# First norm of a two-block transformer step: its conditioning chunks in sixteen buffers, its tiles in PSUM, its time-step matmuls behind 24 units

## The reference

```python
c_act = jax.nn.silu(c)                       # c: (1, 1024)
mod = c_act @ ada_w + ada_b                  # ada_w: (1024, 6144)
sh1, sc1, gt1, sh2, sc2, gt2 = jnp.split(mod, 6, axis=-1)
h = rmsnorm(x, mix_pre_g) * (1.0 + sc1) + sh1
proj = h @ w_in                              # 1024 -> z, xbc, dt_raw, sc_b, sc_c, sc_h, gates
xbc = jax.nn.silu(causal_dwconv(xbc, conv_w, conv_b))
dt = jax.nn.softplus(dt_raw + dt_bias)       # 32 heads; the time step of the scan
```

## Time and profile before

| | us |
|---|---|
| median of 3 runs | 1198.6 (1196.49 to 1199.68) |
| profiled execution, its own time | 1196.25 |
| span of its profile | 1194.2 |
| TensorE matmuls busy | 1079.9 (90%) |
| TensorE weight loads busy | 999.0 (84%) |
| GpSimd busy | 722.9 (61%) |
| ScalarE busy | 637.1 (53%) |
| VectorE busy | 600.3 (50%) |
| mean granted TensorE clock | 0.95 of full speed |
| DMA, mean over the span | 189 GB/s |

### The profile page before, as it was taken

How to read it: one execution, slowest core, us unless ns; L and a number is a source line. 1 busy time by engine, 2 the same in 40 slices (tenths; PEclk the granted TensorE clock), 3 DMA queues, 4 the chain that set the end, 5 groups by cost and what they waited for, 6 DMA issues and landing times.

```text
span 1194.2 us, 22510 instructions
## 1 busy us (share of the span) xinstructions
PE 1079.9 (90%) x8161; PEld 999.0 (84%) x8161; DVE 600.3 (50%) x1193; ACT 637.1 (53%) x1106; POOL 722.9 (61%) x332
## 2 busy tenths in 40 slices
PE   3489999889899878999997899998979997999999
PEld 2389999878799867999996799995457586999998
DVE  5777524869964454555523441390137266444400
ACT  2445664255674356666545556736245545666642
POOL 0468888441248754888886387660860034888785
PEclk7699999999999988999998898999969998999999
DMA  8768877555546762777686287547320013555553
GB/s 309 283 214 280 275 278 255 186 201 195 153 148 230 264 212 73 238 225 236 218 263 228 66 272 256 179 129 301 140 72 1 1 58 109 188 181 188 177 184 115
DMA packets 63423, 226.26 MB, mean 189 GB/s; under 512 B 6880, under 2 KB 7936, under 8 KB 63104
## 3 DMA queue, kind: packets, MB, share of 16 engines
q1 hardware_dynamic: 62160, 221.20, 55.0%
q10 hardware_dynamic: 1200, 4.23, 1.1%
HBM read 224.32 MB, written 1.08 MB: 189 GB/s over the span
## 4 chain that ended last, share of the span: by engine, by line
PE 55%; issue 16%; POOL 15%; DVE 8%; ACT 4%; DMA 1%; POOLq 0%; ACTq 0%; DVEq 0%
PE psL L541 51%; POOL WL L468 14%; PE psO L541 3%; DVE CT L1752 1%; DVE CT L1764 1%; ACT R L1457 1%; DMA ring<-wts 1%; DVE adaring L1684 1%; DVE R L1671 1%; PE psS L541 1%; PE psS L872 1%; ACT L955 1%; DVE adaring L1685 0%; DVE X L1767 0%; DVE R L1670 0%
## 5 line engine op out<-in xcount | busy, mean ns | idle before, releaser
L468 POOL TENSOR_TENSOR WL<-ring,WH 128x1024 fp32r<-128x1024 f32 (+1 forms) x282 | 673.1, 2397 | 353.0 <-ACT WH L964 281.9
L541 PE MATMUL psL<-HR,WH 128*128 128x256 f32 x3056 | 557.4, 285 | 21.4 <-DVE HR L1537 8.0
L541 PEld LDWEIGHTS psL<-HR,WH 128*128 128x128 f32 x3056 | 475.4, 191 | 27.9 <-issue 15.9
L541 PE MATMUL psL<-HR,WL 128*128 128x256 f32 x1528 | 433.1, 283 | 0.0
L541 PEld LDWEIGHTS psL<-HR,WL 128*128 128x128 f32 x1528 | 292.1, 191 | 0.0
L964 ACT ACTIVATE WH<-ring 128x1024 fp32r<-128x1024 f32 (+1 forms) x210 | 216.1, 1040 | 142.1 <-PE psL L541 105.4
L541 PE MATMUL psL<-RR,WH 128*128 128x256 f32 x1344 | 241.9, 283 | 6.5 <-DVE RR L1730 3.6
L541 PEld LDWEIGHTS psL<-RR,WH 128*128 128x128 f32 x1344 | 207.6, 189 | 8.2 <-DVE RR L1730 4.0
L541 PE MATMUL psL<-RR,WL 128*128 128x256 f32 x672 | 189.3, 282 | 0.0
L1518 DVE SCALAR_TENSOR_TENSOR adaring<-adaring,psO 128x1024 f32<-128x1024 f32 x96 | 116.3, 1219 | 95.4 <-DMA adaring<-ada_w 86.6
L1793 DVE SCALAR_TENSOR_TENSOR CT<-psL,par,CT 128x254 f32<-128x254 f32 (+1 forms) x176 | 80.8, 480 | 121.7 <-ACT CT L1227 116.4
(11 more groups left out here) (244 smaller groups left out, 1125.6 us busy)
## 6 DMA issues: line engine op xcount, KB each, us to landing
ring<-wts SPq DMA_DIRECT2D x285, 512.0 KB, 4.1
adaring<-ada_w SPq DMA_DIRECT2D x96, 512.0 KB, 4.9
ring<-wts SPq DMA_DIRECT2D x16, 384.0 KB, 3.6
R<-cum_dram ACTq DMA_DIRECT2D x8, 512.0 KB, 4.9
WHF<-wts SPq DMA_DIRECT2D x2, 2048.0 KB, 8.4
ring<-wts SPq DMA_DIRECT2D x8, 288.0 KB, 2.7
WLF<-wts SPq DMA_DIRECT2D x1, 2048.0 KB, 13.7
ring<-wts SPq DMA_DIRECT2D x1, 2048.0 KB, 7.8
```

Source lines behind the costliest of these rows:

```text
L468: nc.gpsimd.tensor_tensor(WL[:, k, 0:n], ring[:, k, 0:n], WH[:, k, 0:n].bitcast(F32), SUB).then_inc(lo_done, 1)
L541: return nc.tensor.matmul(out, lhsT, rhs, start=start, stop=stop)
```

## The change

1. The first sixteen conditioning chunks go to sixteen places in R (`ADA0`), which is unused until the first unit's result, with a semaphore each; their loads wait for nothing. `adaring` serves chunks from 16 on, and 16 to 19 are loaded without a wait.
2. c is loaded broadcast to 128 partitions (`CROW`, 512 KB) and ScalarE writes silu of it to psO; the first diagonals and their matmuls are gone. Parameters are cut earlier: 192 columns (96 KB) first, the rest (1781.5 KB) later under a semaphore of its own.
3. SP's order at the start: CROW, first parameters, chunks 0 to 3, x, 4 to 9, weight 0, chunks 10 to 12, weight 1, chunks 13 to 15, weights 2 and 3, the other parameters, chunks 16 to 19, weights 4 to 7. Then conditioning chunk 20+k after weights 8+2k and 9+2k; the last rounds end with weights 60, 61, conditioning 46, weights 62, 63, conditioning 47.
4. `make_h` writes its scaled tile to one of three psL banks (1 to 3, `first_t`) and reads the root from psS. ScalarE makes two high halves before the tiles and two after.
5. The first units wait for the tiles k by k; the time-step matmuls stand behind unit 23, w_dt's halves behind the tiles, and VectorE's time-step chain behind the 24 convolutions, with conditioning steps 28 to 31 inside it.

```diff
+        ADA0 = [R[:, n * ADA_COLS + (0 if n < 14 else 4096):(n + 1) * ADA_COLS + (0 if n < 14 else 4096)] for n in range(ADA_FIRST)]
+        CROW = R[:, 20480:21504]
...
+        def first_t(j):
+            return psL[:, 1 + j % 3, 0:T]
...
-                if n >= ADA_SLOTS:
+                if n >= ADA_FIRST + ADA_SLOTS:
                     sp.wait_ge(ada_used, n - ADA_SLOTS + 1 + i * per)
...
+            sp.dma_start(CROW, c_row.rearrange("a b -> (a b)").partition_broadcast(P)).then_inc(c_in, 16)
             sp.dma_start(par[:, 0:PAR_FIRST], par_in[:, 0:PAR_FIRST]).then_inc(par_in_sem, 16)
             for n in range(4):
+                load_first(n)
+            sp.dma_start(X[:, :, :], x_t).then_inc(x_in, 16)
+            for n in range(4, 10):
+                load_first(n)
+            load(0)
+            for n in range(10, 13):
+                load_first(n)
+            load(1)
+            for n in range(13, 16):
+                load_first(n)
+            load(2)
+            load(3)
+            sp.dma_start(par[:, PAR_FIRST:NPAR], par_in[:, PAR_FIRST:NPAR]).then_inc(par2_in, 16)
+            for n in range(16, 20):
                 load_ada(n)
-            sp.dma_start(X[:, :, :], x_t).then_inc(x_in, 16)
-            for n in range(4, 16):
-                load_ada(n)
-            for c in range(SLOTS):
+            for c in range(4, 8):
                 load(c)
-            sp.dma_start(par[:, PAR_FIRST:NPAR], par_in[:, PAR_FIRST:NPAR]).then_inc(par_in_sem, 16)
-            load_ada(16)
-            load_ada(17)
             with sp.Fori(0, 7, 1) as i:
                 for k in range(4):
-                    load(4 + 2 * k, i, 8)
-                    load(5 + 2 * k, i, 8)
-                    load_ada(18 + k, i, 4)
-            for c in (60, 61):
-                load(c)
-            load_ada(46)
-            load_ada(47)
-            for c in (62, 63):
-                load(c)
+                    load(8 + 2 * k, i, 8)
+                    load(9 + 2 * k, i, 8)
+                    load_ada(20 + k, i, 4)
...
-            cond_rows(DIAG1, 1)
             pe.wait_ge(sq_ready, 1)
             stat("stat_mix", sq_at, 8)
+            linear8("in1", 0, 24, h_hi, h_lo, from_count(h_ready, 0))
             pe.wait_ge(wdt_ready, 1)
             out = scratch("dt")
             for k in range(KD):
-                pe.wait_ge(h_ready, k + 1)
                 wh, wl = (WDT[:, part, k * 32:(k + 1) * 32] for part in range(2))
                 last = triple(out[0:32, 0:T], wh, wl, HH[:, k, :], HL[:, k, :], k == 0, k == 7)
             last.then_inc(s_done, 1)
-            linear8("in1", 0, 64, h_hi, h_lo)
+            linear8("in1", 24, 40, h_hi, h_lo)
...
+            A(csil[:, :], pv("c_2"), ACT.Silu).then_inc(csil_ready, 1)
+            act.wait_ge(c_in, 16)
+            A(psO[:, :, :].rearrange("p a b -> p (a b)"), CROW, ACT.Silu).then_inc(cbc_ready, 1)
...
+            A(sbank("stat_mix")[:, 0:T], RS[:, 0, :], ACT.Exp, scale=-0.5).then_inc(rs_ready, 1)
+            for c in range(2):
+                high(c)
+            make_hh(mod[:, 0:8], 0, first_t)
+            for c in range(2, SLOTS):
+                high(c)
+            fed[0] = SLOTS
+            act.wait_ge(par2_in, 16)
+            A(WDT[:, 0, :], pv("w_dt"), ACT.Copy).then_inc(wdt_hi, 1)
...
+            units("in1", 24, 4, z_bank)
             act.wait_ge(dtw_ready, 1)
             A(dts[:, 4, :], dts[:, 2, :], ACT.Ln).then_inc(dtl_ready, 1)
+            units("in1", 28, 12, lambda k, u, i: z_bank(k, u, i, 4))
...
+            make_h(mod[:, 0:8], lead[:, 0:8], sbank("stat_mix")[:, 0:T], 0, first_t)
+            dve.wait_ge(t_ready, 8)
+            dve.sem_inc(s_free[SCRATCH["stat_mix"] % 2], 1)
+            dve.wait_ge(par2_in, 16)
             dve.wait_ge(wdt_hi, 1)
             V.tensor_tensor(WDT[:, 1, :], pv("w_dt"), WDT[:, 0, :].bitcast(F32), SUB).then_inc(wdt_ready, 1)
```

More of the change, by code:

```diff
@@ L39 @@
 ADA_COLS = 1024
-ADA_GROUPS = 6 * D // ADA_COLS
+ADA_FIRST = 16
 class Stream:
@@ L137 @@
 PAR_SPEC = [
-    ("c", 8), ("c_2", 8), ("ada_b", 48), ("mix_pre_g", 8), ("ones", P), ("ident", P), ("w_dt", KD * HEADS1),
-    ("mix_post_g", 8),
+    ("c_2", 8), ("ada_b", 48), ("mix_pre_g", 8), ("ones", P),
+    ("ident", P), ("w_dt", KD * HEADS1), ("mix_post_g", 8),
     ("xconv_w", 4 * NXBC), ("xconv_b", NXBC), ("dskip", 16), ("ssd_norm_g", 16), ("sconv_w", 24),
@@ L281, in build @@
         ada_arrived = [sem(f"ada_arrived{i}") for i in range(ADA_SLOTS)]
+        ada_first = [sem(f"ada_first{i}") for i in range(ADA_FIRST)]
         ada_used = sem("ada_used")
+        c_in, par2_in = sem("c_in"), sem("par2_in")
         diag_ready, cbc_ready, mod_ready = sem("diag_ready"), sem("cbc_ready"), sem("mod_ready")
@@ L1520, in _, with make_h @@
             dve.wait_ge(cbc_ready, 1)
-            for n, first in ((0, 8), (8, 0)):
-                with st.repeat(2, 0) as i:
-                    for kk in range(4):
-                        ada_step(n + kk, mod[:, bass.ds(i * 4 + (first + kk), 1)], i, 4)
-            def make_h(shift, gains, rs, base):
+            for n in range(ADA_FIRST):
+                first = n + 8 if n < 8 else n - 8
+                dve.wait_ge(ada_first[n], 16)
+                V.scalar_tensor_tensor(ADA0[n], ADA0[n], 1.0, cond, MUL, MUL, accum_out=mod[:, first:first + 1]
+                                       ).then_inc(ada_used, 1)
+            def make_h(shift, gains, rs, base, t_at=None):
+                slots = 3 if t_at else 4
                 for j in range(KD + 1):
                     if j < KD:
-                        if j >= 4:
-                            dve.wait_ge(h_ready, base + j - 3)
-                        V.scalar_tensor_tensor(CT[:, j % 4, :], X[:, j, :], gains[:, j:j + 1], rs, MUL, MUL
-                                               ).then_inc(t_ready, 1)
+                        if j >= slots:
+                            dve.wait_ge(h_ready, base + j - slots + 1)
+                        V.scalar_tensor_tensor(t_at(j) if t_at else CT[:, j % 4, :], X[:, j, :], gains[:, j:j + 1], rs, MUL,
+                                               MUL).then_inc(t_ready, 1)
                     if j >= 1:
@@ L1719, in _ @@
                 if m == 4:
-                    diagonals(DIAG2, 8)
+                    diagonals(DIAG2)
                 u = u0 + m
```

109 lines of the change are left out of this document (52 added, 57 removed).

## The result

| | before | after |
|---|---|---|
| median, measured together | 1199.14 us (1196.49 to 1202.33) | 1156.54 us (1153.14 to 1166.93) |
| profiled execution, its own time | 1196.25 us | 1153.14 us |
| span of its profile | 1194.2 us | 1151.2 us |

The ratio is 0.9662, with an interval of 0.9634 to 0.9689: 40.5 us gained by the ratio, 42.6 by the medians. The forecast was 1177.5 us, with a range of 1171 to 1188. The change has moved the code by some lines, so before's L541 is L554 in after, L468 is L481, L964 is L976, L1518 is L1542 for the first sixteen steps and L1536 for the rest, L1532 and L1537 are L1552 and L1557, and L1610 is L1632.

The account below looks back on a forecast made before the run. Matmuls into psL carry 51% of the span; gains were sought where TensorE is not streaming. Terms 13.1 + 5.9 - 2.8 + 3.7 = 19.9 us: 1176.4, or 1178.7 against the median; taken 1177.5, range 1171 to 1188.

Parts of the forecast that it names:

- 1, last early chunk: Start: conditioning chunk 15 usable at 31.0 instead of 32.94, with DMA at 405 GB/s; 1.9 us gained.
- 2, to the first tile: Between last early chunk and first tile: the time-step subtraction leaves the path; 0.3 us gained.
- 3, tiles: Normed tiles on VectorE: 7.1 us instead of 15.4, no low half beside them, one SBUF operand; 8.3 us gained.
- 3, last tile to unit 3: First unit follows the tiles k by k, 0.6 us behind the last instead of 2.84; 2.6 us gained.
- 4, units 3 to 23: in1 units until 24: TensorE's stall for VectorE's convolution and its slow clock go; 5.9 us gained.
- 5, units 23 to 60: 24 time-step matmuls now stand in a full stream behind unit 23; 2.8 us lost.
- 6, units 60 to 63: End of in1: weights 62 and 63 no longer queue behind conditioning load 47; 3.7 us gained, bounds 2.0 to 4.2.
- the late convolution: Rival: a third collision makes VectorE's first convolution late for unit 4; 3 us lost, 1181 us; chance 0.13.
- After in1 every stage should be the same and only shifted: Sign to look for: stages behind in1 keep their times, and the gain made before them stays.
- The slow feed: Rival: DMA at the start stays at the ring's 330 GB/s; gain 10 us, 1187 us; chance 0.20.
- The broadcast row: Rival, slower than before: the condition row's load, first in the queue, delays everything; 1217 us if it takes 40; chance 0.05.
- The gain is not kept: Rival: what comes early waits later for something that does not move; 1195 us; chance 0.04.

Follow-up runs that it names:

- f2: after with an unused tensor of 32 bytes per partition ahead of X, giving all but some small buffers before's addresses; 1179.19 us, ratio 0.9826.
- h3: f2 with before's load order at the end of in1: conditioning chunk 47 ahead of weight chunks 62 and 63; 1184.14 us, ratio 0.9899.
- D = 320 and 448: D: distance WH to HR modulo 512. 320: after with 128 bytes ahead of X, 1172.1 us; 448: before with 224 bytes, 1182.39 us, and i2.
- i1: after with 512 unused bytes per partition ahead of X; 1156.03 us, ratio 0.9638 to before.
- i2: after with 256 unused bytes per partition ahead of X; 1155.99 us in one run.

## Why the prediction was wrong, point by point

Of f2, which is the change at before's addresses, every term can be read from the last chunk's step, the first tile, the last low tile, the convolution starts of units 3 and 23 and the products of units 60 and 63:

| term | forecast | f2 | after |
|---|---|---|---|
| 1, last early chunk | 1.9 (at 31.0) | 2.1 (30.87) | 1.3 (31.64) |
| 2, to the first tile | 0.3 | 0.3 | 0.4 |
| 3, tiles | 8.3 | 8.5 | 8.5 |
| 3, last tile to unit 3 | 2.6 | 2.8 | 3.2 |
| 4, units 3 to 23 | 5.9 | 5.9 | 8.3 |
| 5, units 23 to 60 | -2.8 | -2.7 | 0.1 |
| 6, units 60 to 63 | 3.7 | 3.8 | 3.8 |
| sum, at the product of unit 63 | 19.9 | 20.7 | 25.5 |
| behind it | 0 | -2.3 | 17.6 |
| profiled execution | 1176.4 us | 1177.87 us | 1153.14 us |

- **Parts 1 to 4 held** in their sizes, each within 0.3 us in f2. Where I chose between bounds (405 GB/s between 330 and 413; no price for a PSUM operand; no price for weight 4 and the late convolution) the trace of after shows 404 to 429 from 9 us on, 0.47 to 0.48 us and no stall. The last early chunk starts between 30.29 and 31.82 in the fourteen kernels with this feed, and between 32.13 and 34.71 in five with before's: a spread that no part of the sum had, and which hides differences under 1.5 us. In part 3 the reason was only half the right one: the text names the low halves and the SBUF operands, and not the 4.13 us for which VectorE waited for ScalarE. The size came out because the 7.1 us of undisturbed tiles, read from the trace, left out both losses.
- **Part 5** is -2.7 as forecast. **Part 6** has the forecast size as a difference of two whole kernels, but only 2.3 of its 3.8 belong to the order of the last loads (h3); the rest came with something else in the change, which I did not follow. The forecast had put all of it down to the order, so its 3.7 is in part luck.
- **The step that failed** is one that was not a term of the sum: "After in1 every stage should be the same and only shifted", and with it the 2.84 us per unit that was carried over to every stage. I had read 460 matmuls in 54.2 us as what TensorE takes, a property of the instruction. It is one of several cadences: after has 2.72 us per unit. The diff had this in plain sight, as `("c", 8)` dropped from the parameter table, and I counted its bytes of DMA but not where the buffers behind it would go. The missing term is the 22.7 us between f2 and after; without it, 1179.19 stands against 1177.5, and in the range. (That f2 came so near is in part luck: of its 20.7 us at unit 63 the profiled execution loses 2.3 behind it, which the sum did not have either.)
- **The rivals.** The slow feed did not come (404 to 429 GB/s). The broadcast row was used at 5.95, near the 6 reckoned, but it was not free: from 3 to 9 us DMA moved 320 GB/s in after and 361 in f2, where before has 389. By an estimate, (389 - 320) x 6 us / 405, that is 1.0 us in after and 0.4 in f2. It is also most of the spread of the last early chunk: the six kernels that moved 319 to 338 GB/s in these 6 us have it at 31.45 to 31.82, and the eight with 351 to 368 at 30.29 to 30.98. The Trainium skill, "DMA: Bandwidth & Descriptors", section "Where 436 GB/s comes from", with its 358 GB/s for loads from HBM, is not what this trace of a single core shows; "Perfetto Trace Analysis", section "Roofline", which lets a single core draw up to about 435, agrees with 429. The late convolution is the rival that came nearest: two collisions, as reckoned (1.40 and 2.42 us), and unit 0's first tap at 45.74, where 45.9 was forecast. "The gain is not kept" did not come: 20.7 us at unit 63 are 18.4 at the end of f2, and 20.9 by its ratio.
- **Range and chances.** The range was built of feed, stalls and order, the resources that the diff names. No width of these holds a time that comes from the layout. The chance of 0.91 for faster came out, and the reason given for it covers half of the gain.

What stays open: what in the chip the distance of weights and tiles touches (TensorE's weight load against its own moving read, or reads of other engines beside them) was not separated; nor what picks the cadence at D = 320 and 448, where both are seen; nor whether 192 is fast with weights and tiles both elsewhere; nor whether RR, which moves along with HR and feeds a quarter of the matmuls (2016 of 8157), has a best distance of its own. No version faster than after was found: i1 and, in its one run, i2 equal it.

## What to carry to other kernels

Before you forecast a change to a kernel that is bound by matmuls, list every buffer whose address it moves, and compare only kernels with the same addresses; a padding tensor puts them back and separates layout from order in one run. A cadence read from a full stream holds for that layout alone: count matmuls in a few far windows, also in stages that the change does not touch. And list both what runs beside a slow stretch and what it waits for: here GpSimd's low halves cost VectorE's tiles nothing if they are apart, or if one operand lies in PSUM, but as much again was lost in a wait for ScalarE, which only the order or an earlier feed removes.
